# Output products of the differential heads as three f16 products, and ScalarE's copy of the transposes moved ahead of the exponentials

## The chip, the cores and the metric

The kernel runs on one core of a Trainium2 chip. The metric is the device time of one execution in microseconds (us). A program for one core has no other cores to wait for. The engines are TensorE (PE in the rows, its weight loads PEld), VectorE (DVE), ScalarE (ACT), GpSimd (POOL) and SyncE (SP), which issues the weight transfers.

## The reference, cut to what matters

Sequence 512, width 1024. Two layers of a first block (feed-forward, gated recurrence and windowed attention, feed-forward) are followed by two layers of a second block. Its differential attention is what is changed here:

```
logits = einsum('bqhmd,bkhmd->bhmqk', q_blk, k) * scale + bias     # 4 heads, 2 maps m each
p = softmax(logits, axis=-1)
attn = p[:, :, 0] - lam * p[:, :, 1]
out = einsum('bhqk,bkhd->bqhd', attn, v)                           # v: 512 keys x 128 per head
out = rmsnorm(out, subln_w) * (1.0 - lam_init)
```

Everything is float32. Beside it the layer has a retention of four heads, a pooling branch and an output projection.

## The kernel before

Nearly all large products are made of float32 values that are split into two f16 numbers, a high part and a low part (what the high part leaves over). A product is then three f16 matmuls: high by high, low by high, high by low. Values are scaled before the split (weights by 1024, activations by `ASCALE` = 64), and scaled back when PSUM is read.

The input projection of the second block is cut into 18 units (`MIX2_ORDER`: aq, ak, av, aq, ak, ag, av, ag, cu, cu, bq, bk, bv, bg, ...), each of 256 columns. A unit is 4 parts of 12 matmuls with 512 columns (or 24 with 256). ScalarE makes the high part of the unit's weights (`hi`, L1917), VectorE the low part (`lo`, L1132), in a pair of slots that alternate.

Between the parts TensorE does the small work of the attention, in steps q. `MIX2_SLOTS` gives unit 3 step 0, and each later unit two steps. Steps 0 to 15 are 4 heads times 4 blocks of 128 queries. For step q:
- TensorE: `scores2(q)` (6 f16 matmuls, L912) into the two banks of the step's parity, `pm[0]`, `pm[1]` or `pm[2]`, `pm[3]`.
- VectorE: `softmax2(q)`: adds the bias (L1684, twice), the maximum (L1686), its negative (L1688, signals `mx_ready`).
- ScalarE: two exponentials with sums (L2264, signals `ex_done`).
- VectorE: `probs2(q)` (L1694 to L1699, signals `p_ready`): the difference of the two maps, 128 queries by 512 keys.
- TensorE, in step q+1: `transpose2(q)` (L933), four f32 transposes back into the step's first bank.
- ScalarE: `taken(q)` (L2252) copies them to `AT`, f32, and signals `pt_ready`. `scores2(q+2)` waits for that, since it overwrites the bank.

In steps 5, 9, 13 and 17 a head is complete, and `head_out2` (L939) multiplies `AT` by `dV`: 16 f32 matmuls of 128x128 by 128x128 into `pm[1]`. ScalarE copies the result to `tc` (L2272), sums its squares (`head_squares`, L2110) and takes the root (L1936, another activation table). VectorE scales it one step later (`scale_head`). In steps 7, 11, 15 TensorE transposes it (`head_turn`, L725), ScalarE copies that to `r_post` (`copy_scale`, L2246, signals `o_cp`) and VectorE finishes (`head_post2`). `scores2(8)` and `scores2(12)` wait for `o_cp`, since the turned head lay in `pm[1]`. The same `head_out2` serves the four retention heads later.

Each engine works its list strictly in the order written. In VectorE's, the work of a step is `softmax2`, then `scale_head` if due, then `between` (the low weight part in a unit's first step, the evacuation of the unit's result in its second), then `probs2`. In ScalarE's, a unit begins with `hi` (and the two silu for ag, bg, cg), then its two steps follow.

`dV` is written by VectorE alone (`normed`, L1206, four pieces of 256 columns); `aq` and `ak` are already split (`SPLIT2`): ScalarE writes the high part (`part_high`, L2295), VectorE the low part (L1779).

Of the kernel before, what the change touches and what calls it, by code (L numbers as in the profile page):

```python
# [19 lines left out]
ALU = mybir.AluOpType  # L20
# [3 lines left out]
P = 128  # L24
T = 512
# [66 lines left out]
U_FFN, U_MIX = FFN_SLOTS - 1, MIX_ALL - 1  # L92


SPLIT2 = ("aq", "ak")
SS = 1.0 / (ASCALE * ASCALE)


# [3 lines left out]
def evacuated(n, by_act, order=MIX_ORDER):  # L102
# [14 lines left out]
PER2 = dict(split=24, land0=32 * 12, land1=32 * 12, hi_split=24, unit_done=23, evac=MIX2_DVE, evac_a=MIX2_ACT, pre_act=2, act_done=2, y_park=4, y_done=4,  # L117
            dec_pre=4, dec_done=4, sc_done=16, mx_ready=16, ex_done=16, p_ready=16, pt_done=16,
            pt_ready=16, o_rc=8, o_done=8, o_sq=8, o_rt=8, o_rb=8, o_cp=8, m_ready=12, rot_ready=2, rot_land=64, dup_land=32, ret_done=16, ret_ready=16, pw_land=16,
            part_hi=4,   # L120
            pool_sum=1, pool_in=4, pool_done=4, pool_free=1, x_ready=4, rx=4, xn_ready=4, tp_done=8, hh_ready=8, h_ready=8)


# [56 lines left out]
def build_program(nc, a, out):  # L180

    with ExitStack() as ctx:
# [77 lines left out]
        dec, dec2 = f32(86.25, TW), f32(89.75, TW)  # L260
        AT = f32(93.25, NB, T)
        (daq_hi, daq_lo), (dak_hi, dak_lo) = ((v[:, 0::2], v[:, 1::2]) for v in (f16(0, 8, T), f16(8, 8, T)))

        rel_hot, rel_row = f32(0, 2 * T)[0:32], f32(85, 2 * T)[0:A_HEADS]
        rel_tab = f32(8, A_HEADS)[0:32]
# [84 lines left out]
        toep_land = sem("toep_land")  # L350
        rot_ready = sem("rot_ready")
        part_hi = sem("part_hi")
        rot_land = sem("rot_land")
        ak_land = sem("ak_land")
        dup_land = sem("dup_land")
# [14 lines left out]

        def halves2(kind, part, banks):

            dst = {"aq": (daq_hi, daq_lo), "ak": (dak_hi, dak_lo)}
            out_hi, out_lo = dst[kind]
            scale = DS * ASCALE * (0.125 if kind == "aq" else 1.0)
            if kind in ("av", "bv"):
                cols = slice(part * 256, part * 256 + 256)
                return [(out_hi[:, b:b + 2, cols], out_lo[:, b:b + 2, cols], banks[b // 2][:].rearrange("p (b c) -> p b c", b=2), scale) for b in (0, 2)]
            return [(out_hi[:, 2 * part + e], out_lo[:, 2 * part + e], banks[e][:], scale) for e in range(2)]
# [105 lines left out]
        def _(pe):  # L485
# [447 lines left out]
                    last = nc.tensor.transpose(pm[2 * (i % 2)][:, c], src[:, c], ident[:])  # L933
                last.then_inc(pt_done, 1)

            def head_out2(ps, v_tok, hd):
                for b in range(NB):
                    for kb in range(NB):
                        last = nc.tensor.matmul(ps[:, b * P:(b + 1) * P], AT[:, kb, b * P:(b + 1) * P], v_tok[:, kb, hd * P:(hd + 1) * P],  # L939
                                                start=kb == 0, stop=kb == NB - 1)  # L940
                last.then_inc(o_done, 1)

            def retention_scores(hd):
# [11 lines left out]
            def mixer2_slot(q):  # L955

                if q in (5, 9, 13, 17):

                    pe.wait_ge(pt_ready, t.next("pt_ready", 4))
                    pe.wait_ge(p_ready, t.now("p_ready"))  # L960
                    if q < 17:
                        pe.wait_ge(p_ready, t.now("p_ready") + 1)
                    else:
                        pe.wait_ge(o_cp, t.next("o_cp"))
                    head_out2(pm[1], dV, (q - 5) // 4)
                if 1 <= q <= 16:
                    transpose2(q - 1)
                if q in (7, 11, 15):
                    head_turn(pm[1], tc[:, (q - 7) // 4 % 2])
                if q == 19:  # L970
                    head_turn(pm[3], tc[:, 1])
                if q in (6, 10, 14, 18):
                    pe.wait_ge(o_sq, t.next("o_sq"))
                hd, step = divmod(q - RET_SLOT, 2)
                if 0 <= hd <= B_HEADS and step == 0:
                    if hd > 1:
                        pe.wait_ge(o_cp, t.next("o_cp"))
                    if hd:
                        pe.wait_ge(o_sq, t.next("o_sq"))
                    else:  # L980
                        pe.wait_ge(rot_ready, t.next("rot_ready", 2))
                    if hd < B_HEADS:
                        retention_scores(hd)
                if 0 <= hd < B_HEADS and step == 1:
                    pe.wait_ge(ret_ready, t.next("ret_ready", NB))
                    if hd % 2 == 0:

                        pe.wait_ge(evac, t.at("evac", 2 + evacuated(MIX2_ORDER.index(("bv", hd // 2)) + 1, False, MIX2_ORDER)))
                    if hd:
                        head_turn(pm[1], tc[:, (hd - 1) % 2])  # L990
                    head_out2(pm[0], bV, hd)
                if q == POOL_SLOT:
                    pe.wait_ge(pw_land, t.next("pw_land", 16))
                    pe.wait_ge(pool_in, t.next("pool_in", 4))
                    head_turn(pm[1], tc[:, 1])
                    for gr in POOL_ORDER:
                        if gr == 1:
                            pe.wait_ge(o_cp, t.next("o_cp"))
                        nc.tensor.matmul(pm[gr][:], poolw[:, gr], cu[:, gr, PAD:PAD + T], start=True, stop=True).then_inc(pool_done, 1)
# [91 lines left out]
        def _(v):  # L1091
# [598 lines left out]
            def probs2(i):  # L1690
# [8 lines left out]
                V.scalar_tensor_tensor(out=Lm[:, 0], in0=Lm[:, 1], scalar=small[:, 7:8], in1=Lm[:, 0],  # L1699
                                       op0=ALU.mult, op1=ALU.add).then_inc(p_ready, 1)  # L1700

            def split_out2(k):
                v.drain()
                V.tensor_copy(out2_hi[k], r_post[:])
                v.drain()
                V.tensor_tensor(out2_lo[k], r_post[:], out2_hi[k], ALU.subtract).then_inc(m_ready, 1)
# [7 lines left out]
            def mixer2_slot(q, between):  # L1714
                hd, step = divmod(q - RET_SLOT, 2)
                if q < 16:
                    softmax2(q)
                if q == 18:
                    v.wait_ge(rot_land, t.next("rot_land", 64))
                    for z, table in ((bqk, K_COS), (swapped, K_SIN)):  # L1720
                        V.tensor_tensor(z, z, cst[:, table:table + T].unsqueeze(1).to_broadcast([P, 4, T]), ALU.mult)
                    v.drain()
                    V.tensor_tensor(bqk, bqk, swapped, ALU.add).then_inc(rot_ready, 1)
                if 0 < hd <= B_HEADS and step == 0:
                    scale_head(tc[:, (hd - 1) % 2])
                if q in (6, 10, 14, 18):
                    scale_head(tc[:, (q - 6) // 4 % 2])
                between()
                if q < 16:
                    probs2(q)  # L1730
                if q == 17:
                    decay_exponents(0)
                if 0 <= hd < B_HEADS and step == 0:
                    v.wait_ge(dec_done, t.next("dec_done"))
                    for b in RET_ORDER[min(hd, 1)]:
                        v.wait_ge(ret_done, t.next("ret_done"))
                        first = 3 * P - b * P
                        V.tensor_tensor(AT[:, b], pm[b][:], dec[:, first:first + T], ALU.mult).then_inc(ret_ready, 1)
                    if hd + 1 < B_HEADS:
                        decay_exponents(hd + 1)  # L1740
                if q == 19:
                    v.wait_ge(pt_done, t.next("pt_done", 2))
                if q in (7, 11, 15, 19):
                    head_post2((q - 7) // 4, small[:, 12:13], dgs[:, (q - 7) // 4])
                if q == 19:
                    v.drain().then_inc(pool_free, 1)
                if 0 < hd <= B_HEADS and step == 1:
                    v.wait_ge(evac_a, t.at("evac_a", evacuated(MIX2_ORDER.index(("bg", (hd - 1) // 2)) + 1, True, MIX2_ORDER)))
                    head_post2(4 + hd - 1, ASCALE, bgs[:, hd - 1])
                if q == POOL_SLOT - 5:  # L1750
                    v.wait_ge(pool_sum, t.next("pool_sum"))
                    for gr, w in enumerate(POOL_WINDOWS):
                        u = cu[:, gr, PAD:PAD + T]
                        V.scalar_tensor_tensor(out=u, in0=wsum[:, gr], scalar=1.0 / w, in1=u, op0=ALU.mult, op1=ALU.subtract).then_inc(pool_in, 1)
# [154 lines left out]
        def _(s_):  # L1909
# [338 lines left out]
            def taken(i):  # L2248

                s_.wait_ge(pt_done, t.next("pt_done"))  # L2250
                b = i % NB
                A.activation(AT[:, :, b * P:(b + 1) * P], pm[2 * (i % 2)][:].rearrange("p (k c) -> p k c", k=NB), ACT.Copy).then_inc(pt_ready, 1)  # L2252

            def mixer2_slot(q):
                ret, step = divmod(q - RET_SLOT, 2)
                if q == RET_SLOT or (1 <= ret <= B_HEADS and step == 1):
                    copy_scale(pm[3 if q == RET_SLOT else 1])
                if q in (8, 12):
                    taken(q - 1)
                if q < 16:  # L2260
                    Lm = tb if q % 2 else ta
# [6 lines left out]
                if ends:  # L2268
                    if k >= 2:
                        s_.wait_ge(m_ready, t.at("m_ready", k - 1))  # L2270
                    s_.wait_ge(o_done, t.next("o_done"))
                    A.activation(tc[:, k % 2], ps[:], ACT.Copy).then_inc(o_sq, 1)  # L2272
                if 1 <= q <= 16 and q not in (8, 12):
                    taken(q - 1)
                if ends:
                    head_squares(tc[:, k % 2])
                if q in (7, 11, 15):
# [270 lines left out]
```

## Time and profile before

| what | us |
|---|---|
| median of 3 runs (2660.72 to 2660.79) | 2660.74 |
| the profiled execution's own time | 2660.73 |
| its span (first to last instruction) | 2658.9 |
| TensorE busy | 2646.9 |
| VectorE busy | 1821.9 |
| ScalarE busy | 1345.8 |

The changed stage is in the two layers of the second block, from about 2060 to 2190 us and from about 2379 to 2509 us of the span. In a row of a timeline the first number is the start, the second the length; a bracket at the end gives the idle time of the engine before it and what ended that. Matmuls are pipelined, so a row of TensorE is longer than the distance to the next one, and the distance is what a matmul costs. A row of the windows gives a stretch and its length, then the busy time of TensorE, its weight loads, VectorE, ScalarE and GpSimd with the number of instructions, then TensorE's granted clock as a share of full speed, the busy share of the DMA engines and GB/s.

### The profile page before, as it was taken

Reading aid. Unit: us, or ns where it says so; the run is one execution under the profiler, and the core shown is the slowest. Engines: PE = TensorE matmul, PEld = TensorE weight load, DVE = VectorE, ACT = ScalarE, POOL = GpSimd, SP = SyncE. Lnnn points to the kernel's source line nnn. Section 1 sums busy time; section 2 is a strip of 40 time slices with the busy share of each in tenths; the row PEclk is TensorE's granted clock in tenths of the full one; section 3 lists DMA queues with packets and bytes.
Section 4 is the critical chain, followed back from the end, with each engine's and each line's share of the span. In section 5 each row is a group of like instructions: output and inputs, shape, how many; then the busy total and the mean of one; then the engine's idle time right before and its main releaser. Section 6 shows DMA issues by size and latency. Waiting matters only on the chain.

```text
span 2658.9 us, 45273 instructions
## 1 busy us (share of the span) xinstructions
PE 2646.9 (100%) x17836; PEld 1738.7 (65%) x17836; DVE 1821.9 (69%) x2792; ACT 1345.8 (51%) x2300; POOL 136.4 (5%) x119
## 2 busy tenths in 40 slices
PE   9999999999999999999999999999999999999999
PEld 6886476654688746886476654688746566465664
DVE  7995385666799628995375656799625886458854
ACT  5664265552566425664265543566424664346452
POOL 1000012100100001000012100100000002000020
PEclk9999999999999999999999999999999999999999
DMA  5443321213344333443322213444433132322312
GB/s 170 112 122 110 123 76 60 92 64 103 96 111 117 120 103 96 111 112 121 116 71 72 92 64 102 126 113 110 126 103 127 64 96 80 111 70 78 111 64 87
DMA packets 313358, 266.23 MB, mean 100 GB/s; under 512 B 8796, under 2 KB 276316, under 8 KB 312576
## 3 DMA queue, kind: packets, MB, share of 16 engines
q1 hardware_dynamic: 310192, 254.31, 31.3%
q10 hardware_dynamic: 2416, 7.84, 1.1%
q0 software_dynamic: 608, 2.11, 0.3%
q8 instruction: 98, 1.61, 0.3%
q14 instruction: 44, 0.36, 0.0%
HBM read 257.40 MB, written 4.21 MB: 98 GB/s over the span
## 4 chain that ended last, share of the span: by engine, by line
PE 97%; DVE 2%; DVEq 0%; DMA 0%; ACT 0%; issue 0%; SPq 0%; ACTq 0%
PE pu L490 15%; PE pu L491 15%; PE pu L492 15%; PE pm L490 6%; PE pm L492 6%; PE pm L491 6%; PE pu L615 6%; PE pu L614 6%; PE pu L613 6%; PE pm L613 2%; PE pm L614 2%; PE pm L615 2%; PE pm L939 2%; PE pm L685 2%; PE pm L912 1%; PE pm L953 1%
## 5 line engine op out<-in xcount | busy, mean ns | idle before, releaser
L1132 DVE SCALAR_TENSOR_TENSOR w_lo<-stage,w_hi 128x2048 f16<-128x2048 f32 (+1 forms) x152 | 342.8, 2255 | 366.9 <-ACT w_hi L1917 363.1
L1917 ACT ACTIVATE w_hi<-stage 128x2048 f16<-128x2048 f32 (+1 forms) x143 | 265.9, 1859 | 526.5 <-PE pm L492 377.9
L490 PE MATMUL pu<-h_hi,w_hi 128*128 128x512 f16 x912 | 346.3, 380 | 0.0
L492 PE MATMUL pu<-h_hi,w_lo 128*128 128x512 f16 x912 | 345.7, 379 | 0.0
L491 PE MATMUL pu<-h_lo,w_hi 128*128 128x512 f16 x912 | 345.7, 379 | 0.0
L492 PE MATMUL pu<-w_hi,arena 128*128 128x512 f16 x512 | 194.1, 379 | 0.0
L490 PE MATMUL pm<-w_hi,arena 128*128 128x512 f16 x512 | 194.1, 379 | 0.0
L491 PE MATMUL pm<-w_lo,arena 128*128 128x512 f16 x512 | 194.1, 379 | 0.0
L490 PE MATMUL pu<-w_hi,arena 128*128 128x512 f16 x512 | 194.1, 379 | 0.0
L491 PE MATMUL pu<-w_lo,arena 128*128 128x512 f16 x512 | 194.1, 379 | 0.0
L492 PE MATMUL pm<-w_hi,arena 128*128 128x512 f16 x512 | 194.0, 379 | 0.0
L2007 ACT ACTIVATE w_hi<-stage 128x768 f16<-128x768 f32 (+1 forms) x140 | 120.1, 858 | 112.7 <-PE pu L615 112.7
L490 PEld LDWEIGHTS pu<-h_hi,w_hi 128*128 128x128 f16 x912 | 90.2, 99 | 112.6 <-issue 22.5
L492 PEld LDWEIGHTS pu<-h_hi,w_lo 128*128 128x128 f16 x912 | 89.2, 98 | 107.6
L613 PE MATMUL pu<-arena 128*128 128x256 f16 x576 | 157.0, 273 | 0.4 <-ACT arena L2021 0.4
L613 PE MATMUL pu<-h_hi,w_hi 128*128 128x256 f16 x576 | 157.0, 273 | 0.2 <-DVE w_lo L1265 0.2
L615 PE MATMUL pu<-h_hi,w_lo 128*128 128x256 f16 x576 | 157.0, 273 | 0.0
L614 PE MATMUL pu<-arena 128*128 128x256 f16 x576 | 157.0, 273 | 0.0
L614 PE MATMUL pu<-h_lo,w_hi 128*128 128x256 f16 x576 | 157.0, 273 | 0.0
L615 PE MATMUL pu<-arena 128*128 128x256 f16 x576 | 157.0, 273 | 0.0
L491 PEld LDWEIGHTS pu<-h_lo,w_hi 128*128 128x128 f16 x912 | 89.2, 98 | 90.3
L1265 DVE SCALAR_TENSOR_TENSOR w_lo<-stage,w_hi 128x1536 f16<-128x1536 f32 x72 | 126.0, 1750 | 0.0
(348 smaller groups left out, 6215.5 us busy)
## 6 DMA issues: line engine op xcount, KB each, us to landing
stage<-in_w_in_dram SPq DMA_DIRECT2D x144, 512.0 KB, 4.6
stage<-in_w_ffn_gate_dram SPq DMA_DIRECT2D x88, 512.0 KB, 4.0
stage<-in_w_ffn_up_dram SPq DMA_DIRECT2D x88, 512.0 KB, 5.2
stage<-in_w_ffn_down_dram SPq DMA_DIRECT2D x80, 512.0 KB, 4.0
stage<-in_w_out_dram SPq DMA_DIRECT2D x40, 512.0 KB, 4.3
stage<-in_w_ffn_down_dram SPq DMA_DIRECT2D x16, 256.0 KB, 4.1
stage<-in_w_branch_hgrn_dram SPq DMA_DIRECT2D x8, 512.0 KB, 3.5
stage<-in_w_branch_attn_dram SPq DMA_DIRECT2D x8, 512.0 KB, 4.5
```

The costliest lines, as they stand in the source:

```text
L490: nc.tensor.matmul(ps, w1, r_hi, start=first, stop=False)
L491: nc.tensor.matmul(ps, w1, r_lo, start=False, stop=False)
L492: return nc.tensor.matmul(ps, w2, r_hi, start=False, stop=last)
L613: nc.tensor.matmul(ps, w1, r1, start=first and k == 0, stop=False, skip_group_check=not first)
L614: nc.tensor.matmul(ps, w1, r2, start=False, stop=False, skip_group_check=not first)
L615: last = nc.tensor.matmul(ps, w2, r1, start=False, stop=k == 3, skip_group_check=not first)
L685: last = nc.tensor.matmul(pm[i % 2][:, b * P // 2:(b + 1) * P // 2].rearrange("p (n l) -> p n l", l=half), lev[:, 2 * pair + 1, b * P:(b + ...
L939: last = nc.tensor.matmul(ps[:, b * P:(b + 1) * P], AT[:, kb, b * P:(b + 1) * P], v_tok[:, kb, hd * P:(hd + 1) * P], start=kb == 0, stop=k ...
L1132: V.scalar_tensor_tensor(out=w_lo[:, s, 0:n], in0=stage[:, s, 0:n], scalar=WSCALE, in1=w_hi[:, s, 0:n], op0=ALU.mult, op1=ALU.subtract).th ...
L1265: V.scalar_tensor_tensor(out=w_lo[:, s, 512:], in0=stage[:, s, 512:], scalar=WSCALE, in1=w_hi[:, s, 512:], op0=ALU.mult, op1=ALU.subtract) ...
L1917: A.activation(w_hi[:, s, 0:n], stage[:, s, 0:n], ACT.Copy, scale=WSCALE).then_inc(hi_split, 1)
L2007: return A.activation(w_hi[:, s, first:last], stage[:, s, first:last], ACT.Copy, scale=WSCALE)
```

## The change

The attention's head outputs become three f16 products, 48 matmuls of 128x128 by 128x128 instead of 16 of f32. For that `av` joins the kinds that are split on evacuation. ScalarE's `taken` now copies the transposes to a f32 buffer `wide` (two halves by parity, in the tile `gp`), and signals `pt_ready` as before. A new `taken_high` makes the high part of it in f16 (signals `pt_hi`), a new `probs_low` on VectorE the low part (signals `pt_lo`). `taken(i)` waits for the low part of step i-2, whose buffer half it takes. The place of `taken(q-1)` in ScalarE's step q is ahead of the exponentials in all steps but 5, 9 and 13; there it is behind them and behind the copy of the output product. Before, it was ahead of them only in steps 8 and 12. `taken_high(q-1)` stands behind the exponentials in all steps. `probs_low(q-1)` stands behind `probs2(q)`, but ahead of it in steps 4, 8, 12 and 16. The output product waits for the low part of its head's last step and for the maximum of the step under way (`mx_ready`) instead of for its probabilities. The retention heads keep the f32 product under the name `head_out_wide`.

```
-SPLIT2 = ("aq", "ak")
+SPLIT2 = ("aq", "ak", "av")
...
+        AT_hi, AT_lo = f16(93.25, NB, T), f16(97.25, NB, T)
+        dV_hi, dV_lo = f16(16, NB, T), f16(20, NB, T)
+        wide = gp[:].rearrange("p (a b) -> p a b", a=2)
...
+            def head_out2(ps, v_hi, v_lo, hd):
+
+                pairs = (AT_hi, v_hi), (AT_hi, v_lo), (AT_lo, v_hi)
+                for b in range(NB):
+                    for kb in range(NB):
+                        for j, (l, r) in enumerate(pairs):
+                            last = nc.tensor.matmul(ps[:, b * P:(b + 1) * P], l[:, kb, b * P:(b + 1) * P], r[:, kb, hd * P:(hd + 1) * P],
+                                                    start=kb + j == 0, stop=kb == NB - 1 and j == 2)
+                last.then_inc(o_done, 1)
...
                 if q in (5, 9, 13, 17):
 
-                    pe.wait_ge(pt_ready, t.next("pt_ready", 4))
-                    pe.wait_ge(p_ready, t.now("p_ready"))
+                    t.next("pt_ready", 4)
+                    pe.wait_ge(pt_lo, t.next("pt_lo", 4))
                     if q < 17:
-                        pe.wait_ge(p_ready, t.now("p_ready") + 1)
+                        pe.wait_ge(mx_ready, t.at("mx_ready", q))
                     else:
                         pe.wait_ge(o_cp, t.next("o_cp"))
-                    head_out2(pm[1], dV, (q - 5) // 4)
+                    head_out2(pm[1], dV_hi, dV_lo, (q - 5) // 4)
...
-                    head_out2(pm[0], bV, hd)
+                    head_out_wide(pm[0], bV, hd)
...
+            def probs_low(i):
+
+                v.wait_ge(pt_hi, t.next("pt_hi"))
+                c = slice(i % NB * P, (i % NB + 1) * P)
+                V.scalar_tensor_tensor(out=AT_lo[:, :, c], in0=wide[:, i % 2].rearrange("p (k c) -> p k c", k=NB), scalar=ASCALE, in1=AT_hi[:, :, c],
+                                       op0=ALU.mult, op1=ALU.subtract).then_inc(pt_lo, 1)
...
                 between()
+                if q in (4, 8, 12, 16):
+                    probs_low(q - 1)
                 if q < 16:
                     probs2(q)
+                    if q not in (0, 4, 8, 12):
+                        probs_low(q - 1)
...
-                A.activation(AT[:, :, b * P:(b + 1) * P], pm[2 * (i % 2)][:].rearrange("p (k c) -> p k c", k=NB), ACT.Copy).then_inc(pt_ready, 1)
+                if i >= 2:
+                    s_.wait_ge(pt_lo, t.at("pt_lo", i - 1))
+                A.activation(wide[:, i % 2], pm[2 * (i % 2)][:], ACT.Copy).then_inc(pt_ready, 1)
+
+            def taken_high(i):
+
+                b = i % NB
+                s_.drain()
+                A.activation(AT_hi[:, :, b * P:(b + 1) * P], wide[:, i % 2].rearrange("p (k c) -> p k c", k=NB), ACT.Copy, scale=ASCALE).then_inc(pt_hi, 1)
...
-                if q in (8, 12):
+                first = 1 <= q <= 16 and q not in (5, 9, 13)
+                if first:
                     taken(q - 1)
...
-                    A.activation(tc[:, k % 2], ps[:], ACT.Copy).then_inc(o_sq, 1)
-                if 1 <= q <= 16 and q not in (8, 12):
-                    taken(q - 1)
+                    A.activation(tc[:, k % 2], ps[:], ACT.Copy, scale=SS if k < A_HEADS else 1.0).then_inc(o_sq, 1)
+                if 1 <= q <= 16:
+                    if not first:
+                        taken(q - 1)
+                    taken_high(q - 1)
```

## Rows read from the trace of the kernel before

**Rows 1.** The page: busy time by engine, and the granted clock in 40 slices.
```profile
PE 2646.9 (100%) x17836; PEld 1738.7 (65%) x17836; DVE 1821.9 (69%) x2792; ACT 1345.8 (51%) x2300; POOL 136.4 (5%) x119
...
PEclk9999999999999999999999999999999999999999
```

**Rows 2.** Waits of TensorE, whole span: total, times, longest; the last of nine.
```profile
PE pm L912 <- ACT r_post L2246: 0.2, 1, 0.2
```

**Rows 3.** Windows of one head each, softmax of step 4 to 8, 8 to 12, 12 to 16.
```profile
2118.51:2148.30 29.79, 29.79 (x173) 15.82 (x172) 24.55 (x42) 20.95 (x39) 0.00 (x0) 1.00 0.23 72
2086.86:2118.51 31.65, 31.65 (x227) 20.93 (x226) 24.68 (x43) 20.84 (x39) 0.00 (x0) 1.00 0.27 90
2148.30:2177.95 29.65, 29.65 (x182) 17.10 (x181) 25.55 (x43) 17.30 (x35) 0.00 (x0) 1.00 0.22 69
```

**Rows 4.** Timeline of TensorE, 2125 to 2130 us: a head's output and what follows.
```profile
2125.44 3.73 PE L939 MATMUL pm<-arena 128*128 128x128 f32 x32
2129.01 0.60 PE L933 MATMUL pm<-ident,ta 128*128 128x128 f32 x4
```

**Rows 5.** Timeline of TensorE, 513 to 516.5 us: first, last of 48, next work.
```profile
513.47 0.22 PE L490 MATMUL pu<-w_hi,h_hi 128*128 128x128 f16 x1
...
516.10 0.22 PE L492 MATMUL pu<-w_hi,h_lo 128*128 128x128 f16 x1
516.15 0.55 PE L708 MATMUL pm<-arena 128*128 128x128 f32 x3
```

**Rows 6.** Groups of weight loads by form: the loads of such units, whole span.
```profile
L490 PEld LDWEIGHTS pu<-w_hi,h_hi 128*128 128x128 f16 x448 | 44.1, 98 | 8.0 <-issue 3.2
```

**Rows 7.** Groups of VectorE by form, 2060 to 2190 us: busy, mean ns | idle before.
```profile
L1132 DVE SCALAR_TENSOR_TENSOR w_lo<-stage,w_hi 128x2048 f16<-128x2048 f32 x9 | 20.6, 2284 | 1.8 <-ACT w_hi L1917 1.8
L1684 DVE SCALAR_TENSOR_TENSOR tb<-pm,arena 128x512 f32<-128x512 f32 x16 | 10.3, 686 | 1.2 <-PE pm L912 0.6 <-issue 0.5
...
L1686 DVE TENSOR_REDUCE small<-tb 128x2 f32<-128x1024 f32 x8 | 9.8, 1219 | 0.6
L1699 DVE SCALAR_TENSOR_TENSOR tb<-tb,small 128x512 f32<-128x512 f32 x8 | 6.0, 751 | 0.7
...
L1697 DVE TENSOR_SCALAR tb<-tb,small 128x512 f32<-128x512 f32 x8 | 3.8, 480 | 0.0
...
L1779 DVE SCALAR_TENSOR_TENSOR arena<-pu,arena 128x512 f16<-128x512 f32 x4 | 2.6, 686 | 0.0
```

**Rows 8.** The same groups of ScalarE.
```profile
L1917 ACT ACTIVATE w_hi<-stage 128x2048 f16<-128x2048 f32 x9 | 17.1, 1905 | 0.5 <-issue 0.5
L2264 ACT ACTIVATE tb<-tb,small 128x512 f32<-128x512 f32 x16 | 11.4, 715 | 15.6 <-DVE small L1688 15.5
...
L2252 ACT ACTIVATE arena<-pm 128x512 f32<-128x512 f32 x16 | 9.5, 597 | 13.0 <-PE pm L933 12.0
L2264 ACT ACT_TABLE_LOAD x6 | 7.7, 1283 | 0.1
```

**Rows 9.** Timeline, pieces of steps 7 to 10.
```profile
2114.83 0.59 ACT L2246 ACTIVATE r_post<-pm 128x512 f32<-128x512 f32 x1
...
2115.61 0.33 PEld L912 LDWEIGHTS pm<-arena 64*128 64x128 f16 x6 [0.42 <-ACT r_post L2246]
...
2118.51 1.29 DVE L1684 SCALAR_TENSOR_TENSOR ta<-pm,arena 128x512 f32<-128x512 f32 x2 [0.17 <-issue]
...
2122.95 0.17 DVE L1694 RECIPROCAL small<-small 128x2 f32<-128x2 f32 x1 [1.61 <-ACTq L2265]
...
2130.25 0.17 DVE L1694 RECIPROCAL small<-small 128x2 f32<-128x2 f32 x1 [0.49 <-ACTq L2265]
...
2133.07 0.69 DVE L1684 SCALAR_TENSOR_TENSOR ta<-pm,arena 128x512 f32<-128x512 f32 x1 [1.19 <-PE pm L912]
```

**Rows 10.** Windows of one microsecond at the start, columns as in rows 3.
```profile
8.00:9.00 1.00, 0.11 (x1) 0.00 (x0) 0.71 (x2) 0.17 (x1) 0.00 (x0) 1.00 1.19 292
...
10.00:11.00 1.00, 1.00 (x7) 0.80 (x6) 0.44 (x2) 0.92 (x3) 0.00 (x0) 0.50 1.19 288
```

More of the change, by code:

```diff
@@ L119 @@
             pt_ready=16, o_rc=8, o_done=8, o_sq=8, o_rt=8, o_rb=8, o_cp=8, m_ready=12, rot_ready=2, rot_land=64, dup_land=32, ret_done=16, ret_ready=16, pw_land=16,
-            part_hi=4,
+            part_hi=6, pt_hi=16, pt_lo=16,
             pool_sum=1, pool_in=4, pool_done=4, pool_free=1, x_ready=4, rx=4, xn_ready=4, tp_done=8, hh_ready=8, h_ready=8)
@@ L352, in build_program @@
         part_hi = sem("part_hi")
+        pt_hi = sem("pt_hi")
+        pt_lo = sem("pt_lo")
         rot_land = sem("rot_land")
@@ L371, in halves2 @@
         def halves2(kind, part, banks):
-            dst = {"aq": (daq_hi, daq_lo), "ak": (dak_hi, dak_lo)}
+            dst = {"aq": (daq_hi, daq_lo), "ak": (dak_hi, dak_lo), "av": (dV_hi, dV_lo)}
             out_hi, out_lo = dst[kind]
@@ L934, in transpose2, with head_out_wide @@
                 last.then_inc(pt_done, 1)
-            def head_out2(ps, v_tok, hd):
+            def head_out_wide(ps, v_tok, hd):
                 for b in range(NB):
```

## Prediction

> **What bounds the kernel.** First the page's busy shares: TensorE is busy 2646.9 of 2658.9 us and its clock is granted in full from end to end [rows 1]. The waits of TensorE confirm it: there are nine groups, and the only one inside the changed stage is 0.2 us, for ScalarE's `r_post` copy [rows 2]. So as long as nobody else is late, an edit is worth exactly what it adds to or takes from TensorE's queue. The question is who is nearly late. The three stretches of one head each (scores of four steps) in the first second-block layer show it: VectorE is busy 24.55 of 29.79 us in the middle one, by the counted time of its instructions, in which the gaps of its drains are not counted [rows 3]. Between step 8 and step 12 (29.79 us) the timeline has three waits that matter: 1.61, 0.49 and 1.19 us, together 3.3 us [rows 9]. VectorE has 3.3 us to spare per head; that is the number that decides.
>
> **The product itself.** Now 16 matmuls (32 passes in the row) of f32 start at 2125.44 and the transposes behind them at 2129.01: 3.57 us [rows 4]. After: 48 matmuls of f16, 128x128 by 128x128. The trace has exactly such a run, in the first block's token unit: first start 513.47, the next other work 516.15, 48 in between, 2.68 us or 0.056 us each, although each has its own weight load of mean 98 ns beside it [rows 5, 6]. Saving 0.89 us per output. It concerns four heads in two layers, 8 outputs: 8 x 0.89 = 7.1 us. The retention outputs keep f32. The worst end is weight loads that no longer hide: 48 x 0.098 = 4.70 us, 1.13 us more than now; I take 0.056 [rows 5], because that run has the same count and shape.
>
> The Trainium skill speaks against this term (TensorE: Matmul & The Clock Gate, Back-to-back issue gap): for pairs of weight load and matmul at 128 columns it gives about 81 ns each. By that rule an output would take 3.9 us and the 8 outputs would cost 2.6 us instead of giving 7.1. The trace does not agree: 56 ns over 48 pairs [rows 5].
>
> **What VectorE gets.** Sixteen low parts per layer, a scalar_tensor_tensor of 512 elements, f16 from f32 and f16. No row has that form from SBUF at 512. Neighbours: 0.75 us (f32 in SBUF), 0.69 us (f16 from PSUM and f16), and 2048 elements at 2.28 us, which at equal rate are 0.57 us [rows 7]. As back-to-back instructions overlap by about 0.07 us I take 0.67 us from start to start, with 0.55 and 0.75 as ends (0.45 if it ran as the 0.48 us of a one-input operation, which I don't take since every two-input row is above). That is 2.7 us per head. The evacuation of `av` changes from 4 pieces (1.4 us in all) to 2 of 0.69: nothing.
>
> **What ScalarE gets.** A second copy per step, `taken_high`, f16 from SBUF: between the PSUM copy of 0.60 and the SBUF exponential of 0.715, starting every 0.6 us with the drain ahead (ends 0.5 and 0.7) [rows 8]. The copy of the transposes moves ahead of the exponentials. ScalarE can bear it before most steps, as it waits 15.6 us over 8 steps for VectorE's maxima [rows 8], and this does free the score banks earlier: they no longer wait on the copy at the end of ScalarE's step. Two high parts of `av` (1.08 us) stand ahead of a weight copy in unit 2, hidden by 7 us of idle VectorE before step 0, and after the square root in unit 6.
>
> **Where it hurts.** Three new orders matter more than the durations.
> 1. In steps 4, 8, 12 VectorE waits for the high part before it computes the probabilities. Now it starts them when the exponentials end (the 1.61 us wait) [rows 9]; then it waits 0.6 us more and runs 0.67 us first. The step's probabilities start some 1.3 us later.
> 2. `r_post` (`copy_scale`) in steps 7, 11, 15 stays at the end of ScalarE's step, behind exponentials and now `taken_high`. Scores of step 8 and 12 wait for it, and there is no slack: the copy starts at 2114.83, ends at 2115.42, the scores start at 2115.61 [rows 9].
> 3. Behind an output product, ScalarE does the exponentials, `tc`, the f32 copy, the high part, squares, square root and a table load of 1.28 us [rows 8]; the next step's exponentials come out later, and with them VectorE's probabilities.
>
> **The walk.** I walk the three queues with these start-to-start times: 12-matmul part 2.59, scores 0.86, transposes 0.44; softmax 2.89 (two of 0.65, reduction 1.3, small ones and drain), probabilities 1.54, low weight part 2.2, evacuation 1.2, scale 0.85, head end 2.1; exponentials 1.62, copies 0.5, weight copy 1.85, read as distances in the timeline, where each next instruction starts about 0.1 us before the end that the groups count [rows 7, 8]; 0.2 us from a last matmul to its reader. With the old orders this gives the softmax of step 8 at 2118.4 and of step 12 at 2148.2 (trace 2118.5, 2148.3) and no TensorE wait, so it describes the stage. With the new ones:
> - Steps 1 to 4: softmax 4 starts at 2088.4 instead of 2086.7; probabilities 4 at 2094.2 instead of 2091.1. Low part 3 is ready at 2094.2 and the output product starts at 2095.4, so that one has 1.2 us of slack and stalls nothing.
> - Exponentials 5 start 1.8 us late, the f32 copy of step 4 with them: scores 6 wait 0.6 us.
> - Softmax 7 starts at 2112.1 (was 2109.6), exponentials 7 end at 2116.5, high part, then `r_post` at 2117.7: scores 8 could start at 2115.1 and wait 2.7 us.
> - Second head: VectorE's 29.8 us become 29.8 + 2.7 (four low parts) + 0.7 (the longer wait in step 8) + 1.2 (probabilities 10 wait for exponentials 10, behind squares and table) less the 2.0 us (1.7 in the trace) of its other waits, which its lateness swallows, = 32.4 us. TensorE needs only 29.9 - 0.9 = 29.0, so it stands 3.4 us: 1.4 at scores 10 (f32 copy of step 8) and 2.0 at scores 12 (`r_post`).
> - Third head and end: 1.0 us at scores 14, 1.5 us at the start of unit 12, whose low weight part sits behind VectorE's backlog. After that the rotation and the decay tables have some 4.7 us of room, all used but not exceeded.
>
> Sum per layer 0.6 + 2.7 + 1.4 + 2.0 + 1.0 + 1.5 = 9.2 us. If the exponential's table load runs right behind the square root instead of behind the copies, the same walk gives 8.5. I take 8.8. Both layers have the same rows and queues. Net: 2 x 8.8 - 7.1 = +10.5 us. The profiled execution took 2660.73 (span 2658.9 and 1.8 around it), as the median of 2660.74. Prediction **2671.2 us**, 0.4% slower. With both new costs at their low ends (0.55 and 0.5 us) and the cheaper place of the table load a layer stands 6.8 us, net +6.5; at the high ends (0.75 and 0.7) and the dearer place 10.4, net +13.7. Own range 2667 to 2675.
>
> **Rivals.**
> - *The new work fits and TensorE's saving shows.* It needs stalls under 0.9 us per layer for a gain beyond 0.2%. For it: the copy that frees the score banks comes ahead of the exponentials in 11 more of the 16 steps. Against: 2.7 us of low parts and at least 0.6 of added waiting meet 3.3 us of spare time. Walked with a low part of nothing and a high part of 0.5 us, a layer still stands 2.6 us, at steps 8, 10 and 12, net -1.9. Only with both near nothing is it 2653.6 (all of -7.1) to 2655.
> - *It evens out.* The low part costs 0.45 and the high part 0.5: stalls of 5.9 per layer, net +4.6, 2665.4. The turning point of the whole change is 3.6 us per layer; 6.2 us per layer is where it becomes slower by 0.2%.
> - *Weight loads don't hide* in the f16 product, at 0.098 us a pair: 8 outputs cost 8 x 1.13 = 9 us instead of giving 7.1, with the stalls 2687, or something between if some hide. Against it stands the run of 48 pairs [rows 5]. The Trainium skill's figure for such pairs (same page and section) would put it at 2681; the trace disagrees as above.
> - *The clock falls.* At the start of the program, after a microsecond with 0.11 us of TensorE work, the granted clock is 0.50 in the microsecond from 10 on [rows 10], the 1.2 GHz level instead of 2.4. If it lasts some 3.4 us, half of that is lost. With each of the eight waits above 1.2 us paying 1.7 us, 14 us more: 2685. Against it: work around these waits is dense, there it was not.
>
> **Chances.** Stalls as walked or near, net +6 to +14: 0.75. Evens out, -5 to +5.3: 0.11 (its upper half nearer). Faster: 0.06. Weight loads 0.04, clock 0.04, both slower. So faster 0.06, same 0.11, slower 0.83; 0.2% (5.3 us) is about what a measurement can tell from no change. Range 2665 to 2677: it leaves out faster, half of the even case, both dear rivals and a tail of the likeliest.
>
> **What the profile after would show.** Head outputs of the attention: 384 f16 matmuls 56 ns apart, 2.7 us each. TensorE waiting some 17 us in all where it waited none: at the scores of steps 8 and 12 for `r_post`, 10 and 14 for the copy of the transposes, unit 12 for `w_lo`. VectorE's wait ahead of the reciprocal in steps 8 and 12 replaced by one of over 2 us ahead of the low part. VectorE nearly without waits between step 8 and 12, which are 32.4 us apart. Wrong would be: step distances of 29 us (VectorE wasn't full), or low parts under 0.5 us.

## The result and the profile after

The changed kernel takes 2674.65 us (median of 5 runs, 2674.40 to 2674.82), the kernel before 2660.74 in the same comparison: ratio 1.0052, 95% interval 1.0041 to 1.0063, 13.9 us slower. The forecast was 2671.2 us with a range of 2665 to 2677. The profiled execution has a span of 2672.6 us against 2658.9, 13.7 more.

The page of the changed kernel, answering to [rows 1]:

```profile
PE 2644.7 (99%) x17964; PEld 1731.9 (65%) x17964; DVE 1843.4 (69%) x2816; ACT 1368.9 (51%) x2340; POOL 136.5 (5%) x119
```

The span grew by 13.7 us and TensorE's busy time fell by 2.2. The shares hardly move; nothing in them says what happened. TensorE's waits from 2060 to 2520 us do, answering to [rows 2] (total, times, longest):

```profile
PE pm L917 <- ACT r_post L2272: 9.6, 4, 2.7
PE pm L917 <- ACT gp L2280: 5.2, 5, 1.4
PE pu L495 <- DVE w_lo L1147: 3.0, 2, 1.5
```

L917 are the scores, L2272 the copy `r_post`, L2280 the f32 copy of the transposes, L1147 a unit's low weight part. Together they are 17.8 us; the prediction named 17. These are the places that the prediction named, and the counts: `r_post` twice in each layer (scores 8 and 12), the low weights once in each (unit 12). The f32 copy holds scores 6, 10 and 14 in the first layer and 6 and 14 in the second.

The output product, timeline of TensorE, answering to [rows 4]:

```profile
2095.68 2.84 PE L954 MATMUL pm<-arena 128*128 128x128 f16 x48
2098.36 0.60 PE L938 MATMUL pm<-ident,ta 128*128 128x128 f32 x4
```

From first start to the next work 2.68 us instead of 3.57, 0.056 us per matmul. The saving is there in full.

The new pieces on VectorE (the low part) and ScalarE (the high part), groups by form from 2060 to 2200 us, answering to [rows 7, 8]:

```profile
L1721 DVE SCALAR_TENSOR_TENSOR arena<-gp,arena 128x512 f16<-128x512 f32 x16 | 11.0, 686 | 6.0 <-ACT arena L2286 5.9
...
L2286 ACT ACTIVATE arena<-gp 128x512 f16<-128x512 f32 x16 | 10.1, 630 | 2.1 <-issue 0.3
```

The windows from softmax 4 to 8 and from softmax 8 to 12, answering to [rows 3]:

```profile
2122.00:2154.56 32.56, 29.18 (x190) 14.88 (x189) 27.03 (x46) 23.36 (x43) 0.00 (x0) 1.00 0.20 66
2088.55:2122.00 33.45, 30.04 (x233) 19.10 (x232) 27.01 (x47) 24.15 (x45) 0.00 (x0) 1.00 0.26 87
```

The middle head takes 32.56 us (29.79 before). TensorE is busy for 29.18 of them and waits for the rest. The timeline of that head shows who waits for whom, answering to [rows 9]:

```profile
2117.28 0.63 ACT L2286 ACTIVATE arena<-gp 128x512 f16<-128x512 f32 x1
...
2117.81 0.58 ACT L2272 ACTIVATE r_post<-pm 128x512 f32<-128x512 f32 x1
...
2118.45 0.82 PE L917 MATMUL pm<-arena 64*128 64x512 f16 x6 [2.66 <-ACT r_post L2272]
...
2127.19 0.69 DVE L1721 SCALAR_TENSOR_TENSOR arena<-gp,arena 128x512 f16<-128x512 f32 x1 [2.36 <-ACT arena L2286]
...
2135.43 0.82 PE L917 MATMUL pm<-arena 64*128 64x512 f16 x6 [1.27 <-ACT gp L2280]
...
2142.90 0.17 DVE L1709 RECIPROCAL small<-small 128x2 f32<-128x2 f32 x1 [1.06 <-ACTq L2300]
...
2151.00 0.82 PE L917 MATMUL pm<-arena 64*128 64x512 f16 x6 [2.11 <-ACT r_post L2272]
...
2159.75 0.69 DVE L1721 SCALAR_TENSOR_TENSOR arena<-gp,arena 128x512 f16<-128x512 f32 x1 [1.17 <-ACT arena L2286]
```

Scores 8 wait 2.66 us, scores 10 1.27, scores 12 2.11. VectorE's wait in step 8, 1.61 us before, is 2.36 and stands ahead of the low part. In step 12 that wait is 1.17 us, where the prediction said over 2. Between step 8 and step 12 VectorE has one other wait of over 0.25 us, 1.06 in step 10, for the exponentials. So it waits 3.4 us in this head, as much as before (3.3), but now for ScalarE alone.

Where TensorE stands relative to the kernel before can be read by subtracting the starts of the same operation in the two timelines. In the first layer TensorE falls behind or gains, place by place: +0.16 us at the transposes of step 3, -0.89 at each output, +0.83 at scores 6, +2.73 at 8, +1.34 at 10, +2.17 at 12, +1.19 at 14, +1.67 around unit 12. That is 10.1 us of standing against 3.6 of saving, +6.5 us. The second layer comes to +7.1 (10.7 against 3.6), together 13.6, the difference of the spans (13.7). Of the 10.7 us, 1.64 are no wait but work at a lower clock (see *The rivals* below).

### The profile page after: what moved, and what is told of

Same layout as the page of the kernel before. It is cut to its first block, busy times and chain, and to the rows that moved or that the text cites. A ratio compares the mean times of both kernels' runs of the same rounds, so it can differ in the third digit from the quotient of the medians.

```text
span 2672.6 us, 45655 instructions
## 1 busy us (share of the span) xinstructions
PE 2644.7 (99%) x17964; PEld 1731.9 (65%) x17964; DVE 1843.4 (69%) x2816; ACT 1368.9 (51%) x2340; POOL 136.5 (5%) x119
## 3 DMA queue, kind: packets, MB, share of 16 engines
q0 software_dynamic: 608, 2.11, 0.3%
## 4 chain that ended last, share of the span: by engine, by line
PE 90%; DVE 5%; ACT 2%; DVEq 2%; issue 1%; ACTq 1%; DMA 0%; SPq 0%
PE pu L495 13%; PE pu L496 13%; PE pu L497 13%; PE pm L495 6%; PE pm L496 6%; PE pm L497 6%; PE pu L619 6%; PE pu L620 6%; PE pu L618 6%; PE pm L618 2%; PE pm L619 2%; PE pm L620 2%; PE pm L690 2%; PE pm L944 1%; DVE small L1701 1%; DVE w_lo L1147 1%
## 5 line engine op out<-in xcount | busy, mean ns | idle before, releaser
L1147 DVE SCALAR_TENSOR_TENSOR w_lo<-stage,w_hi 128x2048 f16<-128x2048 f32 (+1 forms) x152 | 344.1, 2264 | 362.4 <-ACT w_hi L1943 358.7
```

The source lines that it names most:

```text
L1147: V.scalar_tensor_tensor(out=w_lo[:, s, 0:n], in0=stage[:, s, 0:n], scalar=WSCALE, in1=w_hi[:, s, 0:n], op0=ALU.mult, op1=ALU.subtract).th ...
```

## The experiments

All ratios are to the kernel before, run on the same chip; it took 2660.80, 2660.79 and 2660.76 us (medians) in the three groups (the first four, the next four, the last three). The changed kernel was not run again in these groups, so a difference to it is taken to the 2674.65 us above. Theory V claims that VectorE has no room left and that TensorE stands because of what is added to VectorE; the rivals differ by experiment. The walk is the prediction's step-by-step timing of the three queues.

**The product alone.** The edit to the changed kernel, in essence:

```
-                pairs = (AT_hi, v_hi), (AT_hi, v_lo), (AT_lo, v_hi)
+                pairs = (AT_hi, v_hi), (AT_hi, v_lo), (AT_hi, v_hi)
...
-                A.activation(wide[:, i % 2], pm[2 * (i % 2)][:], ACT.Copy).then_inc(pt_ready, 1)
+                A.activation(AT_hi[:, :, b * P:(b + 1) * P], pm[2 * (i % 2)][:].rearrange("p (k c) -> p k c", k=NB), ACT.Copy, scale=ASCALE).then_inc(pt_ready, 1)
```

`taken_high` and `probs_low` are gone, and TensorE's waits and the place of `taken` are as before the change.

> The f16 product and the split of av alone: ScalarE copies the transposes straight to AT_hi in f16, at its old place, and the output product takes high by high, high by low and high by high again, so the low part of the probabilities is left out and nothing is added to VectorE or ScalarE but the split of av. Theory V (the loss comes from VectorE's low parts): 8 outputs save 0.89 us each, no stall, 2653.6 us. Rival P (the f16 product does not pay in its place, through weight loads or waits of its own): 2660 us or more.

Measured 2654.04 us, ratio 0.9975 (0.9965 to 0.9985), 6.8 us faster. The only wait of TensorE in the two stages is 0.3 us:

```profile
PE pm L917 <- ACT arena L2274: 0.3, 1, 0.3
```

So the f16 product and the split of `av` are worth 6.8 of the 7.1 us that were counted. All of the loss is in the rest of the change: the new pieces on VectorE and ScalarE, the waits that go with them and ScalarE's order. This kernel is faster than both, but it leaves out the low part of the probabilities.

**The order alone.** On the kernel before:

```
-                if q in (8, 12):
+                first = 1 <= q <= 16 and q not in (5, 9, 13)
+                if first:
                     taken(q - 1)
...
-                if 1 <= q <= 16 and q not in (8, 12):
+                if 1 <= q <= 16 and not first:
                     taken(q - 1)
```

> The kernel before with one part of the change: the copy of the transposes ahead of the exponentials in all steps but 5, 9 and 13. Theory V: the copy runs while ScalarE waits for VectorE's maxima, 2660.7 us, no difference that can be measured. Rival O (the moved copy holds back the exponentials, and that is what starves TensorE): part of the loss appears here, 2664 us or more.

Measured 2667.06 us, ratio 1.0024 (1.0015 to 1.0033), 6.3 us slower. Theory V's number was wrong here and rival O's right: the moved copy alone is not free. TensorE's waits are at scores 8 and 12 and at unit 12, about 0.9 us each:

```profile
PE pm L912 <- ACT r_post L2246: 3.8, 4, 0.9
PE pu L490 <- DVE w_lo L1132: 1.8, 2, 0.9
```

The cause stands in ScalarE's timeline of step 6. First the kernel before:

```profile
2103.07 0.30 ACT L1936 ACTIVATE r_col<-r_col,eps 128x4 f32<-128x4 f32 x1
2103.39 1.28 ACT L2264 ACT_TABLE_LOAD   x1
2106.02 0.72 ACT L2264 ACTIVATE ta<-ta,small 128x512 f32<-128x512 f32 x1 [1.35 <-DVE small L1688]
```

The table for the exponentials loads right behind the square root, while ScalarE has nothing to do until VectorE's maximum comes. And with the moved copy:

```profile
2106.21 0.60 ACT L2252 ACTIVATE arena<-pm 128x512 f32<-128x512 f32 x1 [2.84 <-PE pm L933]
2106.82 1.28 ACT L2265 ACT_TABLE_LOAD   x1
2108.12 0.72 ACT L2265 ACTIVATE ta<-ta,small 128x512 f32<-128x512 f32 x1
```

The copy waits 2.84 us for the transposes, and the table load, which the program has directly ahead of the exponential, is queued behind it. The exponentials start at 2108.12 instead of 2106.02. The same happens in steps 10 and 14.

**The order with an early table load.** Two more lines on that kernel, an exponential of a single column, which needs the table:

```
                 if ends:
                     head_squares(tc[:, k % 2])
+                if q in (5, 9, 13):
+                    A.activation(zero[:, 1:2], zero[:, 0:1], ACT.Exp)
```

> The kernel before with the moved copy alone (as e2_order_alone), and one exponential of a single column right behind the square root of a head's output in steps 5, 9 and 13, so that the activation table for the exponentials loads there. The moved copy alone stood 1.0 us at scores 8, at scores 12 and at unit 12 in each layer, and its trace shows the table load of 1.28 us behind the copy of steps 6, 10 and 14 instead of ahead of it. Theory T (that load is the whole loss of the order): 2660.8 us, as before. Rival O (the copy ahead of the exponentials costs by itself, by its 0.6 us or its wait for the transposes): 2663 us or more.

Measured 2660.54 us, ratio 0.9999 (0.9990 to 1.0008). TensorE has no wait in the two stages, and step 6 shows the load back behind the square root:

```profile
2103.42 1.28 ACT L2279 ACT_TABLE_LOAD   x1
...
2106.73 0.72 ACT L2265 ACTIVATE ta<-ta,small 128x512 f32<-128x512 f32 x1
```

Theory T holds: the place of the table load is the whole loss of the order.

**The early table load in the changed kernel.** The same two lines.

> The changed kernel with the same early table load. If the parts add up, the 6.3 us of the order come back: 2668.4 us. Theory V (VectorE is the bound of the changed stage, and lateness of ScalarE is shared with it rather than added): the walk gives back only 1.5 us, 2673.2 us.

Measured 2672.81 us, ratio 1.0046 (1.0032 to 1.0059), 1.8 us less than the changed kernel. That is near the walk's 1.5 us and far from the 6.3 of the order alone: where VectorE is late too, most of the two latenesses runs side by side.

**The low part of 8 columns.**

```
-                c = slice(i % NB * P, (i % NB + 1) * P)
+                c = slice(i % NB * P, i % NB * P + 8)
```

(and the input cut alike; the other 120 of each 128 columns are left out).

> The changed kernel, but the low part of the probabilities is made of only 8 of each 128 columns; the rest is left out. All waits and their order stay. Theory V: VectorE gets back some 0.55 us per step, the stalls of a layer fall from about 10.5 to about 6 us: 2665.7 us. Rival S (the stalls come from ScalarE's order alone, r_post behind the high part): at least 2672 us.

Measured 2665.32 us, ratio 1.0017 (1.0008 to 1.0026), 9.3 us less than the changed kernel. Only the length of the low parts changed (0.187 us instead of 0.686 each), not an order or a wait. Taking 8.0 us per layer off VectorE gives back more than the whole product saves, and theory V's number (2665.7) was right. TensorE's remaining waits:

```profile
PE pm L917 <- ACT r_post L2272: 6.8, 4, 1.9
PE pm L917 <- ACT gp L2280: 2.0, 3, 0.8
PE pu L495 <- DVE w_lo L1147: 2.0, 2, 1.0
```

**`r_post` early.** `copy_scale(pm[1])` of steps 7, 11, 15 moved ahead of the exponentials:

```
                 if first:
                     taken(q - 1)
+                if q in (7, 11, 15):
+                    copy_scale(pm[1])
...
-                if q in (7, 11, 15):
-                    copy_scale(pm[1])
```

> The changed kernel with copy_scale moved ahead of the exponentials in steps 7, 11 and 15. Theory V: scores 8 and 12 no longer wait for r_post, but VectorE is as late as before, so TensorE waits elsewhere for it (output products, scores 10 and 14, start of units 8 and 10): 2674.6 us, no change. Rival S: the waits for r_post, 9.6 us in all, vanish: 2665 us.

Measured 2674.22 us, ratio 1.0050 (1.0037 to 1.0064): no change, as theory V said. The largest wait of the changed kernel is gone, and others took its place; that VectorE stands behind them is shown for the last two lines, which name it:

```profile
PE pm L917 <- ACT gp L2280: 7.4, 6, 1.6
PE pu L495 <- DVE w_lo L1147: 7.1, 6, 1.5
PE pm L954 <- DVE arena L1721: 3.8, 4, 1.2
```

This is the run that keeps one from reading the 9.6 us for `r_post` as its price. The move is not free either: the copy (0.6 us) now stands ahead of the exponentials.

**The low part on GpSimd.** ScalarE scales on its first copy, and GpSimd has 16 times per layer:

```
+                        G.tensor_tensor(AT_lo[:, :, c], wide[:, i % 2].rearrange("p (k c) -> p k c", k=NB), AT_hi[:, :, c], ALU.subtract).then_inc(pt_lo, 1)
```

> The changed kernel with the 16 low parts per layer on GpSimd, which is idle there: ScalarE copies the transposes with the factor 64, its high part is a plain copy of that, and GpSimd subtracts. Nothing is left out. Theory V: VectorE has its old work, TensorE waits some 4.3 us per layer less a saving of 3.6 per layer; with the walk's lead over the changed kernel of 9.8 us: 2664.9 us. Rival S (ScalarE's order is what matters): 2672 us or more.

Measured 2677.41 us, ratio 1.0062 (1.0048 to 1.0076), slower than the changed kernel. Theory V missed by 12.5 us. The time is where rival S put it (2672 or more), but not for its reason, as the next run shows. VectorE's groups show why; the probabilities' two operations had 480 and 751 ns before [rows 7]:

```profile
L1714 DVE SCALAR_TENSOR_TENSOR ta<-ta,small 128x512 f32<-128x512 f32 x8 | 11.8, 1471 | 1.0 <-issue 0.4
L1699 DVE SCALAR_TENSOR_TENSOR tb<-pm,arena 128x512 f32<-128x512 f32 x16 | 10.3, 686 | 1.2 <-issue 1.1
...
L1712 DVE TENSOR_SCALAR tb<-tb,small 128x512 f32<-128x512 f32 x8 | 7.6, 953 | 0.0
L1714 DVE SCALAR_TENSOR_TENSOR tb<-tb,small 128x512 f32<-128x512 f32 x8 | 6.9, 862 | 0.7
```

and the timeline has the two together, GpSimd's piece and VectorE's:

```profile
2119.07 1.15 POOL L2503 TENSOR_TENSOR arena<-gp,arena 128x512 f16<-128x512 f32 x1 [5.94 <-ACT arena L2275]
2119.08 1.42 DVE L1712 TENSOR_SCALAR tb<-tb,small 128x512 f32<-128x512 f32 x1
```

A 0.48 us operation takes 1.42 and ends just behind GpSimd's. Eight of one form at +0.72 us, eight of the other at +0.47, and +0.11 on a third are 10.4 us per layer, as much as the 11.0 us of low parts that VectorE was rid of.

**GpSimd with three orders mended** (early table load, high part ahead of the exponentials in steps 4, 8, 12, `r_post` early).

> As e7_gpsimd_low, and three orders on ScalarE: table load early as in e5, the high part ahead of the exponentials in steps 4, 8 and 12, copy_scale ahead of the exponentials in steps 7, 11 and 15. Nothing is left out. The walk gives 2657.8, and as it gave 2.6 us too little for the changed kernel, 2658 to 2660 us: a little faster than before. If GpSimd's pieces are slow (over 2 us) or hold VectorE's back: 2664 us or more.

Measured 2674.39 us, ratio 1.0051 (1.0037 to 1.0065). The walk had 2658 to 2660; the time is on the expectation's other side (2664 or more, if GpSimd's pieces hold VectorE's back). The orders are worth 3.0 us there, and the contention remains (956 ns for the 480 of L1712).

**Two orders of ScalarE mended, low part on VectorE.** On the changed kernel:

```
-                first = 1 <= q <= 16 and q not in (5, 9, 13)
+                first = 1 <= q <= 16 and q not in (5, 6, 9, 10, 13, 14)
                 if first:
                     taken(q - 1)
+                if q in (4, 8, 12):
+                    taken_high(q - 1)
...
-                    taken_high(q - 1)
+                    if q not in (4, 8, 12):
+                        taken_high(q - 1)
```

> The changed kernel, low parts on VectorE, nothing left out, with two orders of ScalarE mended: in steps 6, 10 and 14 the copy of the transposes goes back behind the exponentials (so nothing stands between square root and table load), and in steps 4, 8 and 12 the high part goes ahead of them (so VectorE finds it when it asks). The work on each engine is that of the changed kernel. Theory V with orders on top: 2666.0 us, 8.7 less than the changed kernel (the walk's 2663.3, plus the 2.6 us by which it was low). If VectorE's work alone decides, orders give nothing: 2673 to 2675 us.

Measured 2665.11 us, ratio 1.0018 (1.0009 to 1.0027), 9.5 us less than the changed kernel and still 4.4 more than before. Expected were 2666.0. Nothing is left out, and each engine's work is that of the changed kernel. TensorE's waits in the two stages:

```profile
PE pm L917 <- ACT gp L2280: 8.0, 9, 2.0
PE pm L917 <- ACT r_post L2272: 1.4, 4, 0.4
```

**The high part ahead, alone.** The second of these orders only.

> The changed kernel with the second of these orders alone, the high part ahead of the exponentials in steps 4, 8 and 12. VectorE's wait of over 2 us ahead of the low part there falls to what the exponentials need. Theory V: 0.7 us per head come back and, as the lateness passes on, 4.4 us in all: 2670.2 us. If the wait only hides other lateness: 2674 us.

Measured 2673.20 us, ratio 1.0047 (1.0034 to 1.0061): 1.5 us less, not 4.4. The wait ahead of the low part is gone, as meant. TensorE's waits in the two stages are 13.6 us instead of 17.8, and the whole difference is at the f32 copy (5.2 in the changed kernel):

```profile
PE pm L917 <- ACT gp L2280: 1.0, 2, 0.8
```

So 4.2 us of waits did come back. But the span of its profiled execution, 2670.2 us, is only 2.4 less than the changed kernel's. In that execution the granted clock fell to 0.50 once in each layer (about 2150 to 2154 and 2444 to 2448 us), in the changed kernel's only once, in the second layer (next section). From scores 12 to scores 13 of the first layer, where the added fall is, TensorE took 8.16 us instead of 6.48. These 1.7 us and the 2.4 account for the 4.2 to within 0.1. The profiled execution (2672.05) was the fastest; the other four took 2673.18 to 2673.48 at a mean clock of 0.997 instead of 0.999. Where in them the clock fell was not recorded.

**The low part behind the probabilities in all steps.**

```
-                if q in (4, 8, 12, 16):
+                if q == 16:
                     probs_low(q - 1)
...
-                    if q not in (0, 4, 8, 12):
+                    if q:
                         probs_low(q - 1)
```

> The changed kernel with the low part behind the probabilities in steps 4, 8 and 12 too. VectorE no longer waits for the high part there, but the output product of the next step gets its low part later, and may wait. Theory V: nearly even, 2673.8 us (gain at the probabilities, loss of some 0.5 us at each output product). If the order of these two pieces were what costs: 2668 us or less.

Measured 2673.88 us, ratio 1.0049 (1.0036 to 1.0063), 0.8 us less than the changed kernel. As expected (2673.8): that order alone hardly matters.

## Why the prediction was right, and where it was off

*What bounds.* TensorE until it is starved, and VectorE's list per head as what starves it: right in the walk, which had 32.4 us for the head that took 32.56. But the 3.3 us that the prediction called spare and the number that decides were not all spare. Only the waits of 0.49 and 1.19 us [rows 9] could be swallowed, 1.7 us. The 1.61 us in step 8 is a wait for ScalarE and came back as 2.36. The sum that comes out is 29.8 + 2.7 (low parts, 4 x 0.686) + 0.75 (step 8) + 1.06 (exponentials of step 10; the walk had 1.2) - 1.7 = 32.6 us. The sign "VectorE nearly without waits" was therefore not met, with 3.4 us of waits; it is VectorE and ScalarE in turn that fill the head.

*The product.* 0.056 us a matmul [rows 5] carried over: 8 outputs of 2.68 us. The 7.1 us are 6.8 by the run with the product alone. The dearer figures (a matmul for every weight load of 98 ns, and the Trainium skill's 81, TensorE: Matmul & The Clock Gate, Back-to-back issue gap) are ruled out in this place too.

*The low part.* Forecast 0.67 us from start to start. The instruction takes 0.686, and in steps 8 to 11 the next one starts 0.60 to 0.85 us after it, 2.9 us for the four. Cutting it gave back 9.3 us (expected 9.0). That the length of VectorE's work is the reason for this part of the loss is thus shown, since nothing else was changed.

*The stalls.* Forecast per layer 0.6, 2.7, 1.4, 2.0, 1.0, 1.5 at scores 6, 8, 10, 12, 14 and unit 12; measured in the first layer 0.83, 2.73, 1.34, 2.17, 1.19, 1.67, and 0.16 at step 3 that the walk had not. The term that was mis-sized is their sum: I took 8.8 us (between 8.5 and 9.2 for two places of the table load), and it is 10.1 in the first layer and 10.7 in the second. That is 3.2 us of the 3.4 by which the forecast is low. In the second layer the waits themselves are about what was forecast: the 10.7 hold 1.64 us by which the lower clock stretched TensorE's work, a cost that the sum left to a rival, and no wait at scores 10. The dearer place of the load was the true one: with the load moved to the other, the kernel is 1.8 us faster.

*The copy moved ahead.* Here a step was wrong, though the total hid it. The prediction said that ScalarE can bear the copy ahead of the exponentials before most steps, and gave the place of the table load 0.7 us per layer. In steps 6, 10 and 14 ScalarE can't bear it: alone, the move costs 6.3 us, by pushing the table load out of the wait in which it was hidden. In the changed kernel most of that runs beside VectorE's own lateness and only 1.8 us of it can be had back by the load alone.

*Where a gain went.* From the product alone (2654.04) to the changed kernel (2674.65) are 20.6 us. The length of the low parts is 9.3 of them by one run, two orders of ScalarE are 9.5 by another. These overlap and need not add. What the 11.1 us are that stay between the product alone and both orders mended (2665.11) is not shown: no run has both orders mended and the low parts shortened. In the trace with both orders mended, TensorE's waits (9.4 us) are all for ScalarE's copies.

*The rivals.* Faster would have needed stalls under 0.9 us per layer; the cheapest run with all the work in place waits 4.7. The clock rival came true in a small way: once in the profiled execution, not eight times. (The prediction's first reading, a clock granted in full from end to end [rows 1], is one of slices of 66 us; its own [rows 10] have 0.50 in one microsecond.) Windows of one microsecond in the second layer of the changed kernel, columns as in [rows 3]:

```profile
2443.00:2444.00 1.00, 0.00 (x0) 0.00 (x0) 0.93 (x4) 0.97 (x2) 0.00 (x0) 1.00 0.00 0
2444.00:2445.00 1.00, 0.98 (x6) 0.21 (x6) 0.92 (x3) 0.00 (x0) 0.00 (x0) 0.68 0.37 67
2445.00:2446.00 1.00, 1.00 (x5) 0.33 (x4) 1.00 (x2) 0.00 (x0) 0.00 (x0) 0.50 1.00 349
2446.00:2447.00 1.00, 1.00 (x4) 0.41 (x3) 0.85 (x3) 0.00 (x0) 0.00 (x0) 0.50 1.08 381
2447.00:2448.00 1.00, 1.00 (x5) 0.37 (x3) 0.84 (x2) 0.00 (x0) 0.00 (x0) 0.61 0.76 252
```

TensorE did nothing for 2.72 us up to 2444 (the stall at scores 8), then the granted clock was 0.50, the level of 1.2 GHz, until after 2447. From scores 8 to scores 9 it took 1.64 us longer than before. But scores 10, which stand 1.34 us in the first layer, do not stand in the second: TensorE would have waited there in any case, so in this place the fall cost about 0.3 us. That is not a rule for other places. In two of the changed kernel's five executions the mean clock was 0.997 instead of 0.998 or 0.999, and they took 0.2 to 0.4 us longer; with the high part ahead, such executions took 1.1 to 1.4 us longer than the one at 0.999. The stall of 2.66 us in the first layer brought no fall. With the early table load in the changed kernel, the clock did fall in the first layer, after a stall of 2.51 us.

## What to carry to other kernels

Before an operation is put on an engine that is only 69% busy over the whole run, look at its real waits within the period that repeats in the stage concerned, and at whom each is for. Here there were 3.3 us per head of 30, but 1.6 of them were a wait for ScalarE's exponentials, which new work behind it does not fill. Into the other 1.7 us went 2.7 us of new work and 1.8 of new waiting, and the head grew by 2.8, whatever TensorE saved. In these traces a table load sits directly ahead of the first instruction that needs it; anything put between the last use of the other table and that instruction, above all something that waits, takes the load out of the time in which it was hidden. And the wait that the profile shows as the longest is not the price of what it waits for: taking away 9.6 us of waits for `r_post` gave 0.4 us.

## What was not expected of the hardware

GpSimd holds VectorE up over SBUF data. A GpSimd subtraction of 128x512 takes 1.16 us, and a VectorE tensor_scalar of 0.48 us that meets it takes 1.42. In the two layers of that trace all 8 of this form that meet a GpSimd piece take 1.42 to 1.43, and the 8 that meet none 0.48. GpSimd's pieces take 1.15 to 1.17 us in 30 of 32 cases, so VectorE bears it. The Trainium skill describes a second SBUF read interface that the two share (VectorE: DVE Perf Modes, Two Vector instructions with no wait between them), used by VectorE for two-input operations and for the single-input ones in a two-port mode; the trace agrees, with both kinds lengthened (480 to 953 and 751 to 1471 ns in the mean) and the softmax's operation with one input in PSUM unchanged at 686, though 14 of these meet a GpSimd piece. And in one of the two layers of the same execution the clock fell after a stall of 2.72 us, and in the other it did not after one of 2.66.
